# Early adaLN chunks on one queue with TensorE's help, more products in split form, and the other chunks spread over later stages

## The reference

```
c_act = silu(c)
for layer in (0, 1):
    mod = c_act @ ada_w[layer] + ada_b[layer]       # 1024 x 6144: shift, scale, gate, twice
    h = rmsnorm(x) * (1 + scale_m) + shift_m
    mix = conv_and_retention(h) if layer == 0 else s5_state_space(h)
    x = x + gate_m * mix
    h = rmsnorm(x) * (1 + scale_f) + shift_f
    x = x + gate_f * (relu(h @ w_fc1)**2 @ w_fc2)   # 1024 -> 4096 -> 1024
x = rmsnorm(x)
# layer 2
proj = rmsnorm(x) @ w_in_2    # gq gk gv gg ga1 fq fk fv ff mq and 3 x 1024 gates
y_gla, y_fox, y_mem = gated linear attention, forgetting attention, attention into mem
x = x + (sum_i sigmoid(bg_i) * (y_i @ w_branch_i)) @ w_out_2
x = x + (silu(h2 @ w_ffn_gate) * (h2 @ w_ffn_up)) @ w_ffn_down
```

## Time and profile before

| | us |
|---|---|
| median of 3 runs (1390.31 to 1395.55) | 1395.38 |
| the profiled execution | 1394.85 |
| its span | 1393.0 |
| TensorE (PE) busy | 1269.5 |
| weight loads on TensorE (PEld) busy | 1135.4 |
| VectorE (DVE) busy | 735.4 |
| ScalarE (ACT) busy | 452.9 |
| GpSimd (POOL) busy | 370.1 |
| first projection starts | 54.89 |
| f1.0 runs from | 226.40 |
| f2.0 runs from | 385.65 |

### The profile page before, as it was taken

How to read it: one execution, slowest core, us unless ns; L and a number is a source line. 1 busy time by engine, 2 the same in 40 slices (tenths; PEclk the granted TensorE clock), 3 DMA queues, 4 the chain that set the end, 5 groups by cost and what they waited for, 6 DMA issues and landing times.

```text
span 1393.0 us, 22876 instructions
## 1 busy us (share of the span) xinstructions
PE 1269.5 (91%) x9992; PEld 1135.4 (82%) x9992; DVE 735.4 (53%) x878; ACT 452.9 (33%) x619; POOL 370.1 (27%) x581
## 2 busy tenths in 40 slices
PE   1699998888999967888999999999999998899999
PEld 1587687777889947878999999668678898799998
DVE  4897985434363438955586543304542165555353
ACT  2221123111123343434555332114155343444341
POOL 7999653455534607810000000000000011000000
PEclk9899999999999988999999999999999999999999
DMA  8963675897765283426245555333333344355461
GB/s 324 365 216 140 226 258 203 328 340 289 280 228 210 100 314 107 130 73 235 100 175 183 186 186 183 109 108 126 113 122 121 121 149 154 121 182 182 143 220 61
DMA packets 118787, 258.08 MB, mean 185 GB/s; under 512 B 5056, under 2 KB 18656, under 8 KB 118560
## 3 DMA queue, kind: packets, MB, share of 16 engines
q1 hardware_dynamic: 86160, 185.78, 37.9%
q10 hardware_dynamic: 27584, 51.01, 10.0%
q0 software_dynamic: 4944, 19.83, 3.9%
HBM read 241.93 MB, written 14.68 MB: 184 GB/s over the span
## 4 chain that ended last, share of the span: by engine, by line
PE 71%; DVE 12%; DMA 8%; issue 3%; POOL 3%; ACT 3%; ACTq 0%; DVEq 0%; POOLq 0%
PE bank L1676 71%; DMA ada_slot<-in_ada_w 6%; DVE ada_acc L1189 3%; DVE big L1285 3%; POOL big L722 2%; DVE rstd L1199 1%; DMA memory_kv<-s_tables 1%; POOL big L715 1%; DVE ring_split L1236 1%; DVE h_in L1220 1%; ACT ada_slot_split L802 1%; DMA ring<-in_w_ffn_up 1%; DMA ring<-in_w_ffn_down 1%; DMA ring<-in_w_glu_a 1%; DVE ada_acc L1186 0%
## 5 line engine op out<-in xcount | busy, mean ns | idle before, releaser
L1676 PE MATMUL bank<-h_in,ring 128*128 128x256 f32 x1536 | 351.4, 390 | 7.7 <-ACT h_in L767 7.7
L1676 PEld LDWEIGHTS bank<-h_in,ring 128*128 128x128 f32 x1536 | 297.7, 195 | 53.3 <-issue 10.7
L1676 PE MATMUL bank<-squares_split,ring_split 128*128 128x256 f32 x800 | 226.9, 284 | 0.0
L728 POOL TENSOR_TENSOR y_cat<-y_cat,tmp 128x512 f32<-128x512 f32 x8 | 10.7, 1345 | 552.4 <-DVE tmp L1608 552.4
L1676 PEld LDWEIGHTS bank<-squares_split,ring_split 128*128 128x128 f32 x800 | 154.1, 193 | 0.0
L1189 DVE SCALAR_TENSOR_TENSOR ada_acc<-ada_slot,cact,ada_acc 128x512 f32<-128x512 f32 x168 | 134.0, 797 | 5.9
L1676 PE MATMUL bank<-ada_slot_split,ring_split 128*128 128x256 f32 x432 | 122.2, 283 | 0.0
L1236 DVE TENSOR_TENSOR ring_split<-ring,ada_slot_split 128x2048 fp32r<-128x2048 f32 (+1 forms) x24 | 53.9, 2247 | 62.6 <-ACT ada_slot_split L802 62.6
L1676 PEld LDWEIGHTS bank<-ada_slot_split,ring_split 128*128 128x128 f32 x432 | 82.9, 192 | 0.0
L1676 PE MATMUL bank<-h_in_split,ada_slot_split 128*128 128x256 f32 x256 | 74.9, 293 | 8.3 <-DVE y_cat_split L1612 3.8
L1676 PE MATMUL bank<-one,ada_acc 128*128 128x1 f32 x192 | 29.1, 273 | 56.4 <-DVE mod L1194 35.3
(11 more groups left out here) (391 smaller groups left out, 3084.7 us busy)
## 6 DMA issues: line engine op xcount, KB each, us to landing
ring<-in_w_fc SPq DMA_DIRECT2D x32, 2048.0 KB, 8.2
ada_slot<-in_ada_w ACTq DMA_DIRECT2D x22, 2048.0 KB, 12.4
ring<-in_w_in SPq DMA_DIRECT2D x19, 2048.0 KB, 8.1
ring<-in_w_ffn_gate SPq DMA_DIRECT2D x5, 2048.0 KB, 7.7
ring<-in_w_ffn_up SPq DMA_DIRECT2D x5, 2048.0 KB, 7.8
ring<-in_w_ffn_down SPq DMA_DIRECT2D x5, 2048.0 KB, 7.9
ring<-in_w_out SPq DMA_DIRECT2D x4, 2048.0 KB, 9.1
ring<-in_w_branch SPq DMA_DIRECT2D x3, 2048.0 KB, 7.9
```

Source lines behind the costliest of these rows:

```text
L728: pool.tensor_tensor(merged, merged, tmp3[:, 2 * p:2 * p + 2, :], ALU.add).then_inc(s("mga"), 1)
L1676: return pe.matmul(*args, skip_group_check=True, **kw)
```

## The change

- Chunks 0 to 3 are loaded by SP, one behind the other, behind cols, s5_scal and x; chunk 2 into half of `big`, chunk 3 into the ring's third buffer. Of each of them VectorE sums six slabs and TensorE the other two straight from the chunk. POOL issues no chunk and no constant any more; SP loads ident, rope, scanmask, decay and s5_select behind the panel ag. ScalarE asks for chunk 4 when the panel av has landed, for 5 and 6 behind the shift. The first mean of squares stands ahead of the chunks on TensorE, its reciprocal behind chunk 1 on VectorE.
- f1.0 goes in split form; its first norm splits the input. Chunks 10 to 15 stay in f1.0, each summed in two halves of four slabs between low halves; 16 to 20 go to f2.0, 21 to the gated unit, 22 and 23 to f1.1. State-space rounds 1 to 4 stand behind f1.0's jobs 0, 5, 10, 15, and 5 to 7 behind blocks 1, 3, 5 of f2.0.
- In layer 2 all of gqk, gv, gg, fq, fk, fv, mq and the six gate panels go in split form, as 26 units; ga1 and ff become one split product of 80 rows. The gate results move by 2048 columns in `big`.

```diff
-SW_ADA = 2
+EARLY_ADA = 4
+DVE_SLABS = 6
-ADA_AFTER = {1: 10, 2: 11, 3: 12, 5: 13, 6: 14, 7: 15, 9: 16, 10: 17, 11: 18, 13: 19, 14: 20, 15: 21}
+ADA_AFTER = {3: 10, 6: 11, 8: 12, 11: 13, 13: 14, 15: 15}
+ADA_LOAD_AFTER = {2: 12, 5: 13, 7: 14, 10: 15, 12: 16, 14: 17}
+ADA_HALVES = {0: (10, 0), 1: (10, 1), 2: (11, 0), 4: (11, 1), 5: (12, 0), 6: (12, 1), 7: (13, 0), 9: (13, 1),
+              10: (14, 0), 11: (14, 1), 12: (15, 0), 13: (15, 1)}
+ADA_MOD_BEFORE = {5: 10, 8: 11, 10: 12, 13: 13, 15: 14}
+S5_AFTER = {0: 1, 5: 2, 10: 3, 15: 4}
+SIDE_ADA = {0: 16, 1: 17, 2: 18, 5: 19, 6: 20}
+SIDE_S5 = {1: 5, 3: 6, 5: 7}
...
+        def ada_slot(k):
+            place = big[:, 4096:8192] if k == 2 else ring[2][:, :] if k == 3 else adas[k % 2 if k < 21 else 1][:, :]
...
+        def ada_load(eng, k):
+            if k < EARLY_ADA + 2:
+                job_wait(eng, f"ada{k - EARLY_ADA}")
+            else:
+                eng.wait_ge(s("ada_acc"), k - 1 if k < 22 else k)
+            eng.dma_start(ada_slot(k), ada_source(k)).then_inc(ada_in(k)[0], 16)
...
         # SP
+            for k in range(EARLY_ADA):
+                sp.dma_start(ada_slot(k), ada_source(k)).then_inc(ada_in(k)[0], 16)
...
-                    sp.wait_ge(s("ada_acc"), 2 * ADA)
+                    sp.wait_ge(s("ada_acc"), 21)
...
         # ScalarE
+            squares(0)
+            act.wait_ge(s("panel0"), 16)
+            ada_load(act, 4)
             shift(0)
+            ada_load(act, 5)
             ada_load(act, 6)
...
+            split_high(0)
+            split_high(1)
             squares(1)
             ada_load(act, 11)
             shift(1)
+            split_high(2)
...
             def next_ada(j):
+                if j + 3 < FC:
+                    split_high(j + 3)
+                if j in ADA_LOAD_AFTER:
+                    ada_load(act, ADA_LOAD_AFTER[j])
+                if j in S5_AFTER:
+                    s5_weights_out(S5_AFTER[j])
...
             for b in range(FC2, 8):
                 for u in range(2 * (b - FC2), 2 * (b - FC2) + 2):
+                    split_high(FC + u)
+                    if u in (2, 6, 10):
+                        s5_weights_out(5 + u // 4)
...
                 act.activation(fc2_high(b), big3[:, 4 * b:4 * b + 4, :], ACT.Copy).then_inc(s("b_high"), 1)
+                if 3 <= b < 6:
+                    ada_load(act, 15 + b)
...
+            ada_load(act, 21)
...
                 act.activation(tmp3[:, 2 * p:2 * p + 2, :], ps2(f"gb{p}"), ACT.Sigmoid).then_inc(s("glus"), 1)
+                if p == 2:
+                    ada_load(act, 22)
...
         # VectorE
             ada_mod(9)
             dve.wait_ge(s("mod"), 6)
+            split_low(0)
             residual(0, "wo0", 16)
             norm(1)
+            split_low(1)
+            split_low(2)
...
-            for k in range(10, 23):
-                ada_acc(k)
-                if k > 10:
-                    ada_mod(k - 1)
+            for j in range(16):
+                if j + 3 < FC:
+                    split_low(j + 3)
+                if j in ADA_MOD_BEFORE:
+                    ada_mod(ADA_MOD_BEFORE[j])
+                if j in ADA_HALVES:
+                    k, half = ADA_HALVES[j]
+                    ada_acc(k, 4 * half, 4 * half + 4)
+            ada_acc(16)
+            ada_mod(15)
             for b in range(FC2, 8):
+                split_low(FC + 2 * (b - FC2))
+                split_low(FC + 2 * (b - FC2) + 1)
                 dve.wait_ge(s("b_high"), b - FC2 + 1)
                 tt(big_lo[:, tiles, :], big3[:, tiles, :], fc2_high(b).bitcast(F32), ALU.subtract).then_inc(s("b_low"), 1)
+                if b == 2:
+                    ada_acc(17)
+                    ada_mod(16)
+                    ada_acc(18)
+                    ada_mod(17)
+                elif b == 4:
+                    ada_mod(18)
+                    ada_acc(19)
+                elif b == 5:
+                    ada_acc(20)
+                    ada_mod(19)
+                elif b == 7:
+                    ada_mod(20)
...
                 # gated unit, behind the residual of pair p
+                if p == 1:
+                    ada_acc(21)
+                if p == 2:
+                    ada_mod(21)
...
         # TensorE
+            for j in range(16):
+                project_split(f"f1.0.{j}", j, *input_parts(1), input_ready(1) if j == 0 else no_wait)
...
                 project_split(name, GLU + u, z_hi, z_lo, ...)
+                if name == "ga3":
+                    ada(21)
...
+            def three_nat(out_, x_high, x_low, high, low, start, stop):
+                mm(out_, x_high, high, start=start, stop=False)
+                mm(out_, x_high, low, start=False, stop=False)
+                return mm(out_, x_low, high, start=False, stop=stop)
...
             def gate(j):
-                project(f"bg{j}", panel(f"bg{j // 2}"), 2 * (j % 2), h, no_wait)
+                project_split(f"bg{j}", GATES + j, *h2, no_wait)
```

347 lines of the change are left out of this document (217 added, 130 removed).

## The result

The changed kernel takes 1400.53 us (median of 6 runs, 1398.55 to 1403.81) against 1394.84 for the kernel before on the same chip: ratio 1.0046 [1.0027, 1.0066]. It is 0.5% slower; forecast were 1347 us and a range of 1322 to 1374. The ratio goes by the fast runs alone: one of the six runs of the kernel before took 2137 us. The profiled execution took 1401.68 us (span 1399.9).

What follows compares the result with a forecast made beforehand. TensorE, busy 91% of the span, was taken as the bound. Terms of -9, -45, +22.5, -4, +10, +2.5 and -25 summed to -48 us: forecast 1347 us, range 1322 to 1374.

Steps and rivals of the forecast that it cites:

- First feed-forward: Layer 0's f1.0: cheaper split jobs, fewer chunk jobs and vanished chunk waits, with high and low halves hidden: 45 us less.
- the second step that failed: Layer 0's first feed-forward: GpSimd's state-space weights need no more than before, since GpSimd waits for TensorE up to 27.4 us.
- 27.6: Layer 0's first feed-forward: us saved as four chunk waits of 3.74 and the slower jobs behind them go, 6.9 each.
- The front: Start of f1.0: unit 0's low half ahead of the residual adds 2.3 us, the first job's wait for its input 3.7.
- Rival 1: Low halves cannot overlap GpSimd's rounds, so in the first stage they run in series: 39 us more, 1386; chance 0.03.
- Rival 4: VectorE queues every low half behind a chunk not yet landed, eleven chunks at 12 us each: 1455; chance 0.02.
- Rival 3: ScalarE or transfers bind: panels 15 us late in the first stage, gates giving only half: 1365 to 1380; chance 0.14.
- Rival 2: Chunk 18's late load does no harm and layer 2's projections run at TensorE's pace: 1317; chance 0.10.
- The start: Up to layer 0's first feed-forward: projections begin 16 us sooner, but VectorE's smaller gain remains: 9 us less.
- Second feed-forward: Layer 0's f2.0: chunk 18, asked for late, makes TensorE wait 16.4 us plus 2 for clock; in all 22 more.
- gated unit: Chunk 21's sum and job stand ahead of gb2: wait 8 us, job 0.9, clock 1; 10 more, bounds 2 to 12.
- Layer 2: Projections and gates in split form: ceiling 36 us, less 11 to 14 of waits; 25 less, bounds 10 to 35.

Runs made afterwards that it cites:

- e1: Changed kernel with VectorE reading the results of chunks 10 to 14 earlier, ahead of low halves, in layer 0's first feed-forward: 1379.14 us, ratio 0.9907.
- e15: e1 with most of GpSimd's work in state-space rounds 2 to 4 left out, so those weights are not the reference's: 1372.19 us, ratio 0.9836.
- e4: Changed kernel with chunk 18 loaded ahead of layer 0's second feed-forward, chunks 19 and 20 one block sooner: 1384.52 us, ratio 0.9950.
- e5: Changed kernel with VectorE computing the state-space scalars before it sums chunk 4: 1393.37 us, ratio 1.0005.
- e8: Changed kernel with orders in layer 2 altered (third tile's rows, the gates' logarithms, k_out's copy moved ahead): 1395.66 us, ratio 1.0016.
- e9: Changed kernel with e1, e4, e5 and e8 together, chunk 21 behind the gates and small order edits, round 2 behind job 6: 1339.93 us, ratio 0.9611.
- e16: e14 with two subtractions of 128x1024 per low half instead of four of 128x512: 1327.22 us, ratio 0.9516.
- e7: Changed kernel with the low halves of units 3 to 15 made in four subtractions of 128x512 instead of one: 1401.03 us, ratio 1.0053.
- e14: e12 with the low halves of units 3 to 27, both feed-forward matrices of layer 0, in four subtractions each: 1325.90 us, ratio 0.9521.
- e12: e9 with state-space round 1 ahead of the first feed-forward's first job and round 2 behind job 4: 1333.30 us, ratio 0.9569.

## Why the prediction was wrong

**First feed-forward, the step that failed.** "What takes its place: [...] three halves are made ahead, so both are hidden. Price 0, and 0 to 15 if panels and chunks collide". The sums of busy time were right (VectorE 73 us of work in 110), and so was the job: 5.76 us. But busy sums do not see order. The chunk job's wait for the previous read was never followed through VectorE's queue into ScalarE's, though the prediction does just that in f2.0 and finds its 16 us there. The waits of 3.74 us in the kernel before stood at the same read (`<-DVE mod`), which came behind a sum whose load was late. The change took the late load away and put a low half in its place. Price: 22.9 of the 36 us missing (e1's stage against the changed kernel's).

**GpSimd, the second step that failed.** "POOL's state-space weights need no more than today" was read from its waits before a round, with no look at how long a round would take beside the new neighbour; one round went from 20.5 to 36.3 us and arrived late. The prediction set aside the rule in the Trainium skill ("SBUF — State Buffer", "two separate sides"), by which the pair of ports that GpSimd shares with a VectorE instruction of two SBUF inputs is locked for a whole instruction. It did so on VectorE's chunk steps of 128x512, which hardly stretched, not on the form that the change adds, 128x2048, for which rows stood in the same trace at 454 to 461 us. And it read too much into the rows it had: of the 40 us of the earlier trace rows the two engines are busy at the same time for only some 4, and there it is GpSimd's instructions that stretch, from 0.62 to 0.94 us and a pair from 0.76 to 1.65:

```profile
278.17 0.94 POOL L652 TENSOR_TENSOR tabw<-tabw,early 128x256 f32<-128x256 f32 x1
...
279.08 1.65 POOL L655 TENSOR_TENSOR tabw<-tabw,early 128x128 f32<-128x128 f32 x2
```

For the new form the trace agrees with the rule: GpSimd's 0.6 us become 2.5, and shrink with the pieces, to 1.5 beside 128x1024 and 0.95 beside 128x512. That the lock is the cause is not shown apart from this agreement; that the width of VectorE's instruction sets the delay is. Its price is some 8.2 us in this stage (e15). 22.9 and 8.2 are 31.1 of the 35.8 us between forecast and trace. What is left, 4.6, is still in e15's stage: the `mod` wait of 1.75 with 1.5 in the job behind it, and some 2 by which 27.6 was too large. The fourth of the waits that it counts stands at the very end of the stage (3.68 us, at 384.38), and the slow job behind it is f2.0's first, which the prediction took off there once more, as "-3". The front was priced well: the first job ends 13.0 us after the norm's reciprocal begins, against 12.4 worked out.

**Rival 1** (low halves and GpSimd in series, 39 us) had the mechanism with which the trace agrees and the wrong price: GpSimd's instruction of 0.63 us took 2.55 at most, in the changed kernel a round got 16 us longer at most and not by all of VectorE's work, and GpSimd had slack except at two joins. Its 19.4 us a round was GpSimd's busy time in a window of 40 us; a round took 20.5. **Rival 4** is refuted: over the whole span VectorE waited for a chunk's load 8 times, 51.6 us in all, and once in f1.0, 2.89 us. **Rival 3** too, in the places it named: in f1.0 ScalarE is busy 54 of 146 us and waits for no panel, and the eight gates gave 8.9 us, not half. Elsewhere ScalarE does wait for panels, as it did before: 14.0 us in the gated unit (12.2 before), 7.9 at the last feed-forward (7.9). **Rival 2** is refuted by e4: the late chunk did harm.

**The start.** The term "VectorE's 9 us" measured 4.1: chunk 4, asked for behind av, landed at 55.62. Unit 0's low half took the 2.3 that were counted for it, and 4.1 more went between the convolution and norm 1's reciprocal, at 225.69 for 223.38: some 1.1 in slower products behind TensorE's wait of 11.19, 1.8 at chunk 9's load (5.34 us of wait for 3.57), and 1.2 in wo0's last job, at a lower clock behind a wait of 3.25. e5 shows what was to be had by order alone: 7.7.

**Second feed-forward, right.** 22.5 forecast (its terms, 16.4 + 2 + 2.7 + 3 + 2.4 - 3, sum to 23.5), 24.3 measured, and e4 gives 14.6 of it back with one load. The split of the first wait came out otherwise, 9.73 for chunk 18's job and 4.22 for the block behind it (forecast 11 to 13, and 5). **Tables** -4.8 for -4, **gated unit** +12.3 for +10 with a wait of 5.91 for 8 and 2.3 more behind a panel that landed later (0.5 before), **layer 1** +1.8 for +2.5.

**Layer 2.** "25" was 17.5, inside its bounds of 10 to 35. A gate gave 1.1 for 1.23. The five waits listed sum to 13.7 us, and the sum took off 11. At three of them, for which 10.5 were listed, TensorE waited 12.8, and each lowered the clock behind it, for which nothing was counted. e8 does not close this: how the 7.5 divides among these stays open.

So the signs and sizes of four terms were right and layer 2's sign; the start's was not, and the term of 45 us held 36 of the 55 us of error, two thirds. That e9, 1340, comes near the forecast of 1347 is chance: it has removed waits in f2.0 and the gated unit that the forecast counted as lost, and it still waits 25 us for GpSimd.

## What to carry to other kernels

For every job that a change adds, write down what each of its semaphores waits for, then what stands in front of that in the other engine's queue, and go on until you reach an engine that is free or the one you began with; a shared buffer's read counts as a wait too. Do it for each stage, even where the busy sums are at two thirds: the ring here cost 23 us of its stage with every engine idle part of the time. And judge a contention by rows of the very form that is added, at its width, beside the very neighbour, not by its smaller relatives.

## What the runs showed of the hardware

- A GpSimd instruction of 0.63 us took 2.55 beside a subtraction of 128x2048 on VectorE (after), 1.48 beside 128x1024 (e16) and 0.95 beside 128x512 (e7), while the wide subtraction itself stretched from 2.29 to at most 2.83. With GpSimd's work left out all of them took 2.29 (e15). Cutting the subtraction costs VectorE, beside GpSimd above all: on average in f1.0 2.43 us whole (after), 2.8 in two (e16), 3.3 in four (e14); with GpSimd idle four took 2.49. It paid clear of noise where GpSimd was late and VectorE was not (e14 against e12), and was worth nothing where VectorE is in the ring (e7).
- After waits of 4 to 10 us the granted clock was the lower of its two levels for the next products: eight columns 1.87 us instead of 0.95, and the job behind them 7.5 to 8.3 instead of 5.76 (after). Short waits cost as well: behind 1.75 us the next job took 7.3 (e15). And the mean of the stage was 0.87 with four waits of 4 to 7 us in it (after), 0.94 with two (e1) and 0.95 with none behind the norm (e16).
